# A six-slot ring for fetched expert weights, and a reordered router and dispatch, in a fused decoder layer

## What is computed

```python
def moe_ffn(xn, router_w, router_b, exp_w_gu, exp_b_gu, exp_w_down, exp_b_down):
    logits = (xt @ router_w + router_b)              # xt: (1024, 1024), xn = rmsnorm(h, norm_ffn_g)
    top_val, top_idx = lax.top_k(logits, 4)
    gates = softmax(top_val)
    ...                                              # tokens sorted by expert, padded to blocks
    gu = xb @ w_gu + b_gu                            # per expert: 1024 x 2048
    g = min(gu[:, :1024], 7); u = clip(gu[:, 1024:], -7, 7)
    h = (u + 1) * (g * sigmoid(1.702 * g))
    y = h @ w_down + b_down                          # 1024 x 1024
    ...                                              # y * gate added to the token's row
out = rmsnorm(h + moe, final_norm_g)
```

## Time and profile before

| | |
|---|---|
| median of 3 runs | 2548.66 us (2547.48 to 2551.8) |
| profiled execution | 2544.7 us, its span 2542.7 us |
| PE / DVE / ACT / POOL busy | 93% / 61% / 45% / 16% |
| mean granted PE clock | 0.946 |
| matmul-bound part before the expert loop | 0 to about 903 us |
| last output tile to first expert matmul | about 903 to 956 us |
| expert loop | about 956 to 2500 us |
| memory traffic | 469.6 MB read, 35.3 MB written, 199 GB/s over the span |

### The profile page before, as it was taken

One profiled execution on the slowest core, in us unless ns is written; L12 is line 12 of the kernel. 1 busy time (PEld: TensorE's weight loads), 2 busy tenths in 40 slices (PEclk: granted clock), 3 DMA queues, 4 the chain that ended last, 5 costly groups with the idle time before them and its releaser, 6 DMA issues.

```text
span 2542.7 us, 31708 instructions
## 1 busy us (share of the span) xinstructions
PE 2369.2 (93%) x9597; PEld 1733.8 (68%) x9598; DVE 1550.6 (61%) x1526; ACT 1137.8 (45%) x1078; POOL 401.2 (16%) x344
## 2 busy tenths in 40 slices
PE   7998399989989968999999999999999999999995
PEld 4563274454464556888878888887887787887873
DVE  4536841101052368777776665777778787997783
ACT  4123111022032335565544544556557566774663
POOL 0361400000000001121211211212113022221211
PEclk9989659998999968999999999999999999999998
DMA  5002010130002138787977876879799889997894
GB/s 154 33 1 73 12 42 41 66 133 0 33 34 69 67 111 311 248 312 243 317 242 230 294 227 206 287 259 312 249 300 360 302 288 310 376 371 239 309 347 160
DMA packets 212946, 506.66 MB, mean 199 GB/s; under 512 B 19172, under 2 KB 19400, under 8 KB 211688
## 3 DMA queue, kind: packets, MB, share of 16 engines
q1 hardware_dynamic: 196912, 459.98, 50.4%
q0 software_dynamic: 14032, 45.77, 7.2%
q10 hardware_dynamic: 1960, 0.35, 0.1%
HBM read 469.62 MB, written 35.26 MB: 199 GB/s over the span
## 4 chain that ended last, share of the span: by engine, by line
PE 74%; DVE 9%; issue 5%; DMA 5%; ACT 5%; DVEq 1%; ACTq 0%; SPq 0%; POOLq 0%
PE PS L558 27%; PE PS L861 17%; PE PS L882 11%; PE PS L865 9%; PE PS L889 5%; DMA WA<-in_exp_w_down 4%; DVE WL L1647 2%; DMA WA<-in_exp_w_gu 1%; PE PS L914 1%; PE PS L853 1%; PE PS L818 1%; ACT WH L1165 1%; DVE H L1431 1%; ACT WA L952 1%; ACT YT L952 1%
## 5 line engine op out<-in xcount | busy, mean ns | idle before, releaser
L1647 DVE TENSOR_TENSOR WL<-WA,WH 128x2048 fp32r<-128x2048 f32 x384 | 877.1, 2289 | 302.0 <-ACT WH L1181 113.9
L861 PE MATMUL PS<-WH,XEH 128*128 128x512 f32 x1344 | 361.4, 391 | 0.0
L861 PE MATMUL PS<-WH,XEL 128*128 128x512 f32 x1344 | 361.1, 391 | 0.0
L865 PE MATMUL PS<-WL,XEH 128*128 128x512 f32 x1344 | 347.0, 390 | 0.0
L1165 ACT CAST WH<-WA 128x2048 fp32r<-128x2048 f32 x128 | 243.8, 1907 | 219.3 <-PE PS L865 143.4
L1160 ACT CAST WH<-WA 128x2048 fp32r<-128x2048 f32 x128 | 243.8, 1909 | 198.0 <-PE PS L865 151.5
L1181 ACT CAST WH<-WA 128x2048 fp32r<-128x2048 f32 x124 | 236.6, 1910 | 204.3 <-PE PS L889 181.7
L861 PEld LDWEIGHTS PS<-WH,XEL 128*128 128x128 f32 x1344 | 253.4, 189 | 53.3
L861 PEld LDWEIGHTS PS<-WH,XEH 128*128 128x128 f32 x1344 | 253.5, 189 | 52.1
L865 PEld LDWEIGHTS PS<-WL,XEH 128*128 128x128 f32 x1344 | 253.0, 188 | 52.8
L558 PE MATMUL PS<-WB,YT 128*128 128x512 f32 x512 | 222.9, 593 | 2.6 <-DVE YT L1261 1.6
(11 more groups left out here) (266 smaller groups left out, 2449.3 us busy)
## 6 DMA issues: line engine op xcount, KB each, us to landing
WA<-in_exp_w_gu SPq DMA_DIRECT2D x256, 1024.0 KB, 6.1
WA<-in_exp_w_down SPq DMA_DIRECT2D x128, 1024.0 KB, 7.0
WB<-in_xa_wkv SPq DMA_DIRECT2D x4, 2048.0 KB, 7.8
WB<-in_w_in SPq DMA_DIRECT2D x3, 2048.0 KB, 10.8
y_acc<-H SPq DMA_DIRECT2D x9, 512.0 KB, 2.6
H<-in_x SPq DMA_DIRECT2D x4, 1024.0 KB, 5.9
WB<-in_w_out SPq DMA_DIRECT2D x2, 2048.0 KB, 7.8
WA<-in_x SPq DMA_DIRECT2D x1, 4096.0 KB, 12.1
```

Of the source, the lines that this page charges most:

```text
L861: nc.tensor.matmul(PS[:, 2 * h + t, :], x[:, KT4 * half + k, t * P:(t + 1) * P], WH[:, j % 4, k * HALF:(k + 1) * HALF], start=False, stop= ...
L865: ins = nc.tensor.matmul(PS[:, 2 * h + t, :], XEH[:, KT4 * half + k, t * P:(t + 1) * P], WL[:, j % 4, k * HALF:(k + 1) * HALF], start=Fals ...
L1647: v.tensor_tensor(WL[:, s, :], RAW[:, s, :], WH[:, s, :].bitcast(F32), sub).then_inc(done, 1)
```

## The change

- **Ring.** Six fetched slots: two in H (`RAWH`), free once the loop runs, and the four of WA. Gate/up piece j is in slot (j+2) mod 6, down piece m in slot (m+4) mod 6. SP waits for the low part of the piece six places earlier. Each gate/up piece has a semaphore of its own. OHC moves from H to WL, the scaled OHR (IDR) to WL and HTL, the bias of the down products and the repeated gates to the upper half of H.
- **Router.** PE transposes raw rows of H (waits for `h2_done`); the router weights are multiplied once by the norm's gain (DVE, at n = 1, after `add_out(1, 1)`; PE waits for `rw_done`), and `top` multiplies the logits by 1/rms. DVE's order in each n: both adds, `top(n-1)`, then 1/rms and normed rows.
- **Gates.** One exponential over all eight tiles after the last, then one pass of `gates` over all tiles, behind the tokens' low parts.
- **One-pass products.** Copies in fp32r of the triangle, the ones, the token numbers, MS and CU (made by DVE at `top(6)` and `top(7)`); OH0, OHC and IDR are written as fp32r. `cnt`, `rank`, `idx0` and the list become one pass each.
- **Order up to the first expert.** DVE: low part of weight piece 0, half of OHC, the tokens' low parts, the other half, the gates, then the list. ACT: the tokens' casts ahead of the scaling of OHR. PE: counts loaded ahead of the first transposes.
- Some semaphores are merged (`mem_in` into `x_again`, `d_in` into `par_in`, `gb_in` into `rt_in`, `scatter_go` into `gather_go`), with the waits that this makes longer.

The diff, cut to its core:

```diff
@@ buffers
-        OHC = Hf[:, 0:4096].rearrange("p (n c) -> p n c", c=P)
+        OHC = WLf[:, 2048:2048 + 4096].rearrange("p (n c) -> p n c", c=P)
+        RAWH = Hf[:, 0:2 * KT4 * HALF].rearrange("p (s c) -> p s c", s=2)
+
+        def raw(s):
+            return RAWH[:, s, :] if s < 2 else RAW[:, s - 2, :]
+
+        def raw_gu(j):
+            return raw((j + 2) % 6)
+
+        def raw_dn(m):
+            return raw((m + 4) % 6)
@@ SP
             for j in range(4):
-                wait_filled(sp, ("xt3", 2 * j + 1, 1))
                 sp.wait_ge(xn_out[j], 32)
                 load_gate_up(j, slice(0, 1))
...
                     for s in range(4):
-                        sp.wait_ge(gu_low, 8 * i + s + 1)
+                        if s < 2:
+                            sp.wait_ge(dn_low, 4 * i + s + 3)
+                        else:
+                            sp.wait_ge(gu_low, 8 * i + s - 1)
                         load_gate_up(4 + s, bass.ds(e_i, 1))
...
-                            sp.wait_ge(gu_low, 8 * i + m + 5)
+                            sp.wait_ge(gu_low, 8 * i + m + 3)
                             load_down(m, bass.ds(e_p, 1))
...
+                    for s in range(4):
+                        if s < 2:
+                            sp.wait_ge(gu_low, 8 * i + s + 7)
+                        else:
+                            sp.wait_ge(dn_low, 4 * i + s + 3)
+                        load_gate_up(s, bass.ds(e_n, 1))
@@ PE
-                    tile_transposes("xt3", n - 1, 3, XR0)
+                    tile_transposes("xt3", n - 1, None, H)
...
-                        pe.wait_ge(rt_in, 32)
+                        pe.wait_ge(rw_done, 1)
...
-            end(("cnt",), mm(o[:, 0:E], ones[:], CU[:, L, :], 0, 1))
+            end(("cnt",), mm(o[:, 0:E], ONESR, CUR[:, L, :], 0, 1))
...
-                    ins = mm(o[:, t:t + 1], OH0[:, l, t * P:(t + 1) * P], TOKF[:, l:l + 1], l, L)
+                    ins = mm(o[:, 2 * t:2 * t + 2], OH0[:, l, t * P:(t + 1) * P], TOKR[:, l, :], l, L)
...
+            pe.wait_ge(itm_done, 1)
+            counts = Counts(pe, "pe")
             pe.wait_ge(xg_in, 32)
             token_transposes(0, 2)
             token_transposes(1, 2)
-            pe.wait_ge(hot_done, 1)
-            for l in range(L):
-                pe.wait_ge(idr_done, l + 1)
-                for j in range(TOPK):
-                    n = j * L + l
-                    ins = mm(PS[:, 7, 0:NROW], OHC[:, n, :], OHR[:, n, :], TOPK * l + j, TOPK * L)
+            pe.wait_ge(idr_done, L)
+            for n in range(TOPK * L):
+                if n % (2 * L) == 0:
+                    pe.wait_ge(hot_done, n // (2 * L) + 1)
+                ins = mm(PS[:, 7, 0:NROW], OHC[:, n, :], IDR[n % L // 4][:, n // L, n % 4, :], n, TOPK * L)
             ins.then_inc(list_done, 1)
@@ ACT
-                if n > 1:
-                    gate_exp(n - 2)
...
-            gate_exp(L - 1)
+            act.wait_ge(gexp_in, 1)
+            a(GW, GW, ACT.Exp, s=gexp_done)
...
+            act.wait_ge(ohr_done, 1)
+            for l in range(L):
+                hot = OHR.rearrange("p (j l) r -> p j l r", l=L)[:, :, l, :]
+                nc.scalar.activation(IDR[l // 4][:, :, l % 4, :], hot, ACT.Copy, scale=TOKF[:, l:l + 1]).then_inc(idr_done, 1)
             act.wait_ge(itm_done, 1)
@@ DVE
-                evac(dve, v.tensor_tensor(LG[:, l, :], bank(u)[:, 0:E], RB, add), u, own=True)
+                evac(dve, v.scalar_tensor_tensor(out=LG[:, l, :], in0=bank(u)[:, 0:E], scalar=sm[:, l + 16:l + 17],
+                                                 in1=RB, op0=mul, op1=add), u, own=True)
...
+                if l == L - 2:
+                    d(v.tensor_copy(TRIR, TRI))
+                    d(v.tensor_copy(ONESR, ones[:]))
+                    d(v.tensor_copy(TOKR, TOKF.unsqueeze(2).to_broadcast([P, L, 2])))
+                    d(v.tensor_copy(MSR[:, 0:L - 1, :], MS[:, 0:L - 1, :]))
+                    d(v.tensor_copy(CUR[:, 0:L, :], CU[:, 0:L, :]))
+                if l == L - 1:
+                    d(v.tensor_copy(MSR[:, l, :], MS[:, l, :]))
+                    d(v.tensor_copy(CUR[:, L, :], CU[:, L, :]), ms_done)
...
                     add_out(0, n)
-                if n > 1 and n < L:
-                    gates(n - 2)
+                    add_out(1, n)
+                if n == 1:
+                    dve.wait_ge(rt_in, 48)
+                    dve.wait_ge(iota_done, 4)
+                    dve.wait_ge(tri_done, 1)
+                    tt(RWT, RWT, V[:, V_FFN:V_FFN + K].unsqueeze(2).to_broadcast([P, K, E]), mul, s=rw_done)
+                if n > 0:
+                    top(n - 1)
                 if n < L:
-                    add_out(1, n)
                     rstd(3, n, n)
...
             for j in range(4):
                 dve.wait_ge(gu_high, j + 1)
-                low_weights(j, gu_low)
+                low_weights(j, raw_gu(j), gu_low)
                 if j == 0:
+                    slot_columns(0)
                     for half in range(2):
                         dve.wait_ge(xeh_done, half + 1)
                         low_tokens(half, 2)
+                    slot_columns(1)
+                    gates()
                     dve.wait_ge(list_done, 1)
```

More of the change, by code:

```diff
@@ L173, in build @@
         TRI = wa(11264, P)
+        XELf, HTLf = (x[:, :, :].rearrange("p f s -> p (f s)") for x in (XEL, HTL))
+        WLf = WL[:, :, :].rearrange("p s c -> p (s c)")
+        MSR = XELf[:, 0:L * E].rearrange("p (l e) -> p l e", l=L)
+        CUR = XELf[:, 256:256 + (L + 1) * E].rearrange("p (l e) -> p l e", l=L + 1)
+        TRIR, ONESR = (XELf[:, 544 + P * n:544 + P * (n + 1)] for n in range(2))
+        TOKR = XELf[:, 800:800 + 2 * L].rearrange("p (l r) -> p l r", r=2)
+        GT1 = wa(11776, L, E)
         POSf = YTf[:, 5120:5152]
@@ L193, in build @@
         PRW, PCL = YTf[:, 5280:5312], YTf[:, 5312:5344]
[L194 removed]
+        OHC = WLf[:, 2048:2048 + 4096].rearrange("p (n c) -> p n c", c=P)
+        IDR = [x[:, c:c + 4 * TOPK * NROW].rearrange("p (j l r) -> p j l r", j=TOPK, l=4)
+               for x, c in ((WLf, 6144), (HTLf, 0))]
         OHR = Hf[:, 4096:4096 + TOPK * L * NROW].rearrange("p (n r) -> p n r", r=NROW)
@@ L335, in build @@
         bdn_in, tri_done, fg_in = sem("bdn_in"), sem("tri_done"), sem("fg_in")
-        rg_in = [sem(f"raw{s}_gu_in") for s in range(4)]
-        rd_in = [sem(f"raw{s}_dn_in") for s in range(4)]
+        rg_in = [sem(f"gu{j}_in") for j in range(8)]
+        rd_in = [sem(f"dn{m}_in") for m in range(4)]
         gu_high, gu_low, gu_used = sem("gu_high"), sem("gu_low"), sem("gu_used")
@@ L565, in tile_transposes @@
             def tile_transposes(kind, l, norm, src):
-                pe.wait_ge(xn_done[norm], l + 1)
+                if norm is None:
+                    pe.wait_ge(h2_done, 2 * l + 2)
+                else:
+                    pe.wait_ge(xn_done[norm], l + 1)
                 for h in range(2):
@@ L1132, in _ @@
                 act.wait_ge(rg_in[j], 16)
[L1133 to L1136, removed]
-                nc.scalar.activation(hot, hot, ACT.Copy, scale=TOKF[:, l:l + 1]).then_inc(idr_done, 1)
+                nc.scalar.copy(WH[:, j, :], raw_gu(j)).then_inc(gu_high, 1)
             def keep_tokens(half, tiles):
@@ L1578, in _ @@
                     d(v.memset(ITM3[:, 3, 0:1], 1))
-                if n > 0:
-                    top(n - 1)
             wait_filled(dve, ("rank",))
@@ L1602, in _ @@
             wait_filled(dve, ("idx0",))
-            evac(dve, v.tensor_scalar(IDX0F, bank(("idx0",))[:, 0:2], 1.0, 0.0, sub, ALU.max), ("idx0",), own=True)
+            evac(dve, v.tensor_scalar(IDX0F, bank(("idx0",))[:, 0:4:2], 1.0, 0.0, sub, ALU.max), ("idx0",), own=True)
             d(v.tensor_copy(IDX0, IDX0F), idx0_done)
@@ L1632, in _, with slot_columns, gates @@
             evac(dve, v.tensor_copy(EBS, bank(("eb",))[:, 0:ITEMS + 1]), ("eb",), own=True)
-            v.tensor_tensor(OHC, PCL.unsqueeze(2).to_broadcast([P, TOPK * L, P]),
-                            IOF[:, :].unsqueeze(1).to_broadcast([P, TOPK * L, P]), ALU.is_equal).then_inc(hot_done, 1)
-            gates(L - 2)
-            gates(L - 1)
-            d(v.tensor_copy(GF, GFW), gf_done)
+            def slot_columns(h):
+                ns = slice(2 * L * h, 2 * L * (h + 1))
+                v.tensor_tensor(OHC[:, ns, :], PCL[:, ns].unsqueeze(2).to_broadcast([P, 2 * L, P]),
+                                IOF[:, :].unsqueeze(1).to_broadcast([P, 2 * L, P]), ALU.is_equal).then_inc(hot_done, 1)
+            def gates():
+                dve.wait_ge(gexp_done, 1)
+                d(v.tensor_reduce(MXT[:, 0:L], GW, AX.X, add))
+                d(v.reciprocal(MXT[:, 0:L], MXT[:, 0:L]))
+                tt(GW, GW, MXT[:, 0:L].unsqueeze(2).to_broadcast([P, L, TOPK]), mul)
+                for j in range(TOPK):
+                    tt(GT1 if j else GF, OH4[:, j], GW[:, :, j:j + 1].to_broadcast([P, L, E]), mul)
```

(2 more changed lines are left out.)

95 lines of the change are left out of this document (36 added, 59 removed).

## The result

The changed kernel takes **2510.02 us**, the median of 4 runs (2509.41 to 2511.31), against 2550.23 us (2547.48 to 2551.84) for the kernel before beside it: ratio 0.9844, 95% interval 0.9827 to 0.9861. Its profiled execution took 2509.66 us, its span is 2507.9 us. Predicted were 2509.7 us, 2500 to 2531.

What follows compares the result with a forecast made beforehand. TensorE was taken as the bound, busy eight or nine tenths, with 39 us of the loop lost in eleven one-tile items. Loop 33 plus front 6 gave 2544.7 - 39 = 2505.7, plus 4 = 2509.7 us; range 2500 to 2531.

Steps and rivals of the forecast that it cites:

- The burst items: Five one-tile items coming second after a two-tile item: earlier loads win back almost all their stalls, 24 us.
- The long runs: Six one-tile items in longer runs: 9.5 of 14.5 us won, 5 kept for the DMA rate.
- Rival A: DMA rate limits every run of one-tile items, so only the five bursts are repaired: 2519 us; chance 0.22.
- Rival B: Ring depth does nothing in the loop because WH/WL's four slots gate everything; only 6 us gained: 2543 us; chance 0.07.
- Rival D: Slower: a fuller queue delays GpSimd's indirect transfers, 31 items each stretched by 1.5 us: 2556 us; chance 0.04.
- Rival C: Work before the expert loop gives nothing back, half clock throughout; loop 33 less 1: 2517 us; chance 0.08.
- The front: From the last output tile to the first expert matmul: 6 us gained net, bounds 2 and 9.
- Router: At tile 1 PE waits for router weights scaled after that tile's second add: minus 1.1 us, once.
- The list: Token-list matmuls before the first expert: 32 passes instead of 64, 6 us instead of 9.81.
- The branch: PE's branch between the list and the first expert matmul: its 3.58 us stays.
- SP's first loop load: SP's first load of the expert loop, 5.8 us after the list's end, keeps its distance.
- The carry-over of 4 us: Median 2548.66 lies 4 us above the profiled execution; the same 4 us was added to the forecast.

Runs made afterwards that it cites:

- experiment 1: Changed kernel with its six slots, but each load waits for the low part of the piece four places earlier: 2544.33 us, ratio 0.9985.
- experiment 3: Kernel before with the six-slot ring, its waits and merged semaphores alone; router, products and order up to the first expert as before: 2513.62 us, ratio 0.9862.
- experiment 4: Changed kernel with the router weights scaled ahead of the first sum of tile 0 instead of at tile 1: 2505.42 us, ratio 0.9834.
- experiments 7 and 8: Changed kernel with PE's counts loaded behind the list again: 2510.59 us; changed kernel with list products in two-pass plain fp32: 2513.05 us; one run each.
- experiment 6: Changed kernel with the first item's pieces 4 and 5 loaded right behind its first four, ahead of the list: 2506.78 us, ratio 0.9835.

## Why the prediction was right, and where it was so by luck

**What bounds the loop: right.** The 39 us that were read as lost in eleven items was where the gain came from: 31.1 there and nowhere else. Of its two terms one was too large and one too small. The burst items, second after a two-tile item, fell from 202.6 to 183.6 us: 19.0, not 24. Some 5 us are left in them. The waits of TensorE over the loop, before and then after, name the transposes that wait for the tokens' low parts on VectorE, and they still do, for a tenth of the time:

```profile
PE PS L914 <- DVE XEL L1643: 18.5, 11, 2.4
```

```profile
PE PS L933 <- DVE XEL L1667: 2.0, 5, 0.5
PE PS L872 <- issue: 1.6, 3, 0.6
```

These two account for 3.6 of the 8.3 us by which the loop still exceeds 1377.1. The rest isn't waiting: TensorE is busy for 1381.7 of the 1385.4 us. A one-tile item in which it never stands takes 35.5 us (the one at 1911.90, busy for all of it), so the 35.3 a tile was itself some 0.1 to 0.2 us too short.

The long runs fell from 228.1 to 215.9: 12.1, not 9.5; the term that was kept for the DMA rate did not come, since two slots more let the queue go at 382 GB/s. Sum 31.1 for 33, inside 20 to 39: two misses, of 5 and of 3 us, that partly cancel. VectorE, named as the next thing that might be late, was busy for 34.3 of the 35.5 us and held nothing up there. The next item's first loads, costed at nothing, cost nothing: with the ring alone the first two items took 35.8 and 38.1 us, before 35.7 and 38.2.

**Rival A: refuted.** The items run at 35.5 us and 382 to 383 GB/s, which is the 383 that was worked out as needed for 35.3 us; rival A had them at 36.4. The Trainium skill's figure of 358 GB/s for HBM to SBUF (page "DMA: Bandwidth & Descriptors", section "Where 436 GB/s comes from") would have made them 37.7 us by the prediction's estimate; on this core, with no other at work, the measurement stands above it and decides. Beside the 392 GB/s of the weight queue alone these items leave 2%.

**Rival B: refuted** by experiments 1 and 3. **Rival D:** the scatters landed in 6.3/9.3/11.9 us (6.1/9.1/11.6 before), the fuller queue cost them 0.2 to 0.3 us. **Rival C:** refuted, the front alone is worth 4 us (experiment 1; 3.6 us between the medians of experiment 3 and the changed kernel).

**The front: 6 us predicted, 6.1 found at the first expert matmul, 3.7 where it counts.** By its steps:
- *Router.* Minus 1.1 us predicted, minus 3.4 found. The wait itself was near (1.46 us of standing time); that TensorE then works at the lower clock for a while was left out, and made it three times as dear.
- *Indices, tables, transposes, scalings.* The list would start 3.4 us earlier, before the router's cost. With that cost removed (experiment 4) the gather goes out 8.7 us earlier (9 predicted), the transposes start 6.9 us earlier (8.1 predicted) and the list 3.1 us (146.14 to 143.00). Right.
- *The list.* 6 us predicted, on the thought that the full clock returns in it as it had before; the whole one-pass list ran at the lower clock, 32 x 0.22 = 7.1 us.
- *The branch.* "3.58 us stays" was wrong in the change's favour: it went, with the two-pass list (experiments 7 and 8), and in part because it now begins beside the list's matmuls.
- *SP's first loop load "keeps its distance".* It came 4.5 us after the list instead of 5.8, and that was the miss: the first expert matmul moved up against it by more, the 3.6 us between list and matmul that went, and the first item waited for pieces 4 and 5, 2.2 us. The sum carried no term for it; experiment 6 shows the cost.

So 7.2 - 0.3 - 1.1 - 3.4 + 3.6 = 6.0 us at the first expert matmul, and 2.4 less at the third item. That 949 us was predicted for that matmul and 949.04 came is luck: errors of 2.3, 1.1 and 0.3 us on one side and 3.6 on the other.

**The carry-over of 4 us: wrong.** The sum gave 2505.7 us for the profiled execution; it took 2509.66, 4.0 more. Adding the distance of the median before to its profile, 4 us, covered just that, so that the 2509.7 met the measured median of 2510.02 by luck. After the change median and profile differ by 0.4. The two kernels that fetch four pieces ahead scatter: 2542.8 to 2555.6 in 13 runs of the one before, 2540.1 to 2547.5 in 10 of experiment 1. Those that fetch six scatter by 1.6 to 2.7 us in 4 or 5 runs. Experiment 1 differs from the changed kernel in the depth alone, so the scatter comes with the depth of four; that it comes through the stalls on late pieces is likely and not shown. The distance ought to have been dropped with the four-deep ring: on the median the change is worth more (40 us) than on the profiled executions (35).

## What to carry to other kernels

Lay windows on the repeating items and compare those of one kind: the loss was in eleven items of twenty-nine, five of them behind a two-tile item and its successor, where a full ring had held the DMA back, and six in runs of one-tile items, where the queue ran at its rate but late. Here the first piece of extra depth brought 25.6 us and the second 5.5; a third was not tried. The scatter between runs fell along with it. When a chain is shortened, look at each queue that was merely in time before: a gain at one point is worth only what the next landing or issue leaves of it, and a small wait put into dense TensorE work can cost more than its length, here 3.4 us for 1.46.

## What the runs showed of the hardware

- TensorE stood for 1.46 us amid dense work; 1.9 us after it had resumed its granted clock fell to 0.51 for 3.4 us, and eight matmuls took 5.38 us instead of 3.6. With the wait taken away the clock stayed at 1.00, and 3.4 us were won in all (experiment 4).
- The compare-and-branch into the loop on TensorE took 3.56 to 3.80 us in three instruction streams and 0.35 to 0.45 in eight others; in the three, a 16 KB packet of the queue named instruction lies inside it.
- Loads of 1 MB, with the indirect gathers and scatters beside them, kept 382 to 383 GB/s through four one-tile items on end, 2125.9 to 2269.3 us; over the loop the scatters took 0.2 to 0.3 us longer to land than before.
